# Fetching the next expert's token rows from memory instead of gathering them with matrix products

## The reference

```python
logits = (h @ w_router).astype(jnp.float32)
top_val, top_idx = lax.top_k(logits, TOP_K)
top_w = jax.nn.softmax(top_val, axis=-1)
combine = jnp.sum(jax.nn.one_hot(top_idx, N_EXPERTS) * top_w[..., None], axis=-2)
for e in range(N_EXPERTS):
    y = (jax.nn.silu(h @ w_gate[e]) * (h @ w_up[e])) @ w_down[e]
    out = out + combine[..., e:e + 1] * y
```

## Time and profile before

| what | value |
|---|---|
| median of 3 runs | 1670.8 us (1670.58 to 1673.57) |
| profiled execution, its own time | 1674.03 us |
| its span, first to last instruction | 1672.2 us |
| granted TensorE clock, mean | 0.992 |
| TensorE busy | 1622.5 us, 97% |
| VectorE / ScalarE / GpSimd busy | 578.3 / 501.1 / 49.1 us |
| bytes moved by DMA | 469.96 MB |
| experts, first to last part | 701 to 1655.5 us, 120.2 us from one to the next |

### The profile page before, as it was taken

How to read it: one execution, slowest core, us unless ns; L and a number is a source line. 1 busy time by engine, 2 the same in 40 slices (tenths; PEclk the granted TensorE clock), 3 DMA queues, 4 the chain that set the end, 5 groups by cost and what they waited for, 6 DMA issues and landing times.

```text
span 1672.2 us, 29242 instructions
## 1 busy us (share of the span) xinstructions
PE 1622.5 (97%) x12632; PEld 884.4 (53%) x12632; DVE 578.3 (35%) x820; ACT 501.1 (30%) x745; POOL 49.1 (3%) x33
## 2 busy tenths in 40 slices
PE   6998999999999899999999999999999999999996
PEld 5877788888887777633334334234333333333332
DVE  5877676556787767300100100100100110110101
ACT  5687655444558855300000000000100110010001
POOL 0130000000013000000000000000000000000000
PEclk9999999999999999999999999999999999999998
DMA  9433365555543434399999999999999999999994
GB/s 374 152 130 147 112 241 201 184 185 198 177 164 126 146 132 166 123 385 381 348 370 378 347 376 378 345 388 360 374 376 357 357 391 352 358 385 368 359 386 165
DMA packets 65898, 469.96 MB, mean 281 GB/s; under 512 B 7280, under 2 KB 7536, under 8 KB 9712
## 3 DMA queue, kind: packets, MB, share of 16 engines
q1 hardware_dynamic: 64480, 460.88, 72.5%
q0 software_dynamic: 864, 6.29, 1.0%
q10 hardware_dynamic: 432, 0.96, 0.1%
HBM read 467.05 MB, written 1.05 MB: 280 GB/s over the span
## 4 chain that ended last, share of the span: by engine, by line
PE 81%; DVE 8%; ACT 6%; issue 2%; DMA 1%; SPq 0%; DVEq 0%; ACTq 0%
PE bank L1289 25%; PE turn L1303 12%; PE mid L1289 10%; PE turn L1309 6%; PE bank L503 5%; PE bank L504 5%; PE bank L505 5%; DVE w_lo L498 2%; PE mid L503 2%; PE mid L505 2%; PE mid L504 2%; ACT w_hi L491 2%; PE bank L1201 2%; DMA raw<-in_stream 1%; DVE xT L1542 1%
## 5 line engine op out<-in xcount | busy, mean ns | idle before, releaser
L1289 PE MATMUL bank<-raw,gT 128*32 128x512 f32 (+1 forms) x4096 | 443.5, 567 | 0.8 <-ACT gT L919 0.8
L498 DVE TENSOR_TENSOR w_lo<-raw,w_hi 128x1024 fp32r<-128x1024 f32 x202 | 253.9, 1267 | 154.5 <-ACT w_hi L491 152.8
L1289 PEld LDWEIGHTS bank<-raw,gT 128*32 128x32 f32 x4096 | 129.1, 110 | 265.5 <-issue 255.7
L503 PE MATMUL bank<-w_hi,a_hi 128*128 128x512 f32 (+1 forms) x608 | 242.8, 399 | 15.5 <-DVE w_lo L498 12.0
L491 ACT ACTIVATE w_hi<-raw 128x1024 fp32r<-128x1024 f32 x202 | 211.3, 1056 | 128.0 <-PE bank L505 81.0
L504 PE MATMUL bank<-w_lo,a_hi 128*128 128x512 f32 (+1 forms) x608 | 234.7, 386 | 0.0
L505 PE MATMUL bank<-w_hi,a_lo 128*128 128x512 f32 (+1 forms) x608 | 234.3, 385 | 0.0
L1303 PE MATMUL turn<-raw,hT 128*32 128x512 f32 x1792 | 213.5, 594 | 0.0
L1289 PE MATMUL mid<-raw,gT 128*32 128x256 f32 (+1 forms) x2048 | 188.6, 486 | 0.0
L940 ACT ACTIVATE eh<-bank 128x512 f32<-128x512 f32 (+1 forms) x32 | 17.4, 544 | 455.9 <-PE bank L1289 291.5
L503 PEld LDWEIGHTS bank<-w_hi,a_hi 128*128 128x128 f32 x608 | 116.4, 191 | 41.8 <-issue 15.0
(11 more groups left out here) (226 smaller groups left out, 1377.3 us busy)
## 6 DMA issues: line engine op xcount, KB each, us to landing
raw<-in_stream SPq DMA_DIRECT2D x436, 1024.0 KB, 6.9
wg<-in_gates POOLq DMA_DIRECT2D x2, 2048.0 KB, 10.3
gain<-in_norms POOLq DMA_DIRECT2D x4, 512.0 KB, 4.3
x<-in_x SPq DMA_DIRECT2D x2, 512.0 KB, 6.9
raw<-in_stream SPq DMA_DIRECT2D x2, 512.0 KB, 6.9
out_x<-xn SPq DMA_DIRECT2D x4, 256.0 KB, 2.0
const<-in_consts ACTq DMA_DIRECT2D x1, 752.0 KB, 11.7
gain<-in_norms SPq DMA_DIRECT2D x2, 256.0 KB, 7.1
```

What stands on the lines that cost most here:

```text
L498: nc.vector.tensor_tensor(w_lo[:, h % H, :], raw[:, part % R, lo:lo + HALF], w_hi[:, h % H, :].bitcast(F32), ALU.subtract).then_inc(lo_rea ...
L503: nc.tensor.matmul(out_, s_hi, wh, start=start, stop=False)
L1289: ins = nc.tensor.matmul(bank_[strip(s_), 0:w], gT[:, kt, strip(t_)], w_c, start=kt == 0, stop=kt == KT - 1)
```

## The change

The scaled tokens `xs` are written once to a tensor `tokens` in the chip's memory by GpSimd. For each next expert, TensorE multiplies `sel` with a column that holds each token's number plus one (`number`; two products with one moving column), before part 33. VectorE subtracts one, clips at zero and writes the result as whole numbers into `index` (96 places). GpSimd waits for that, then issues an indirect DMA that fetches 96 rows of 4 KB into `fetched`. Before part 40 TensorE waits for the rows and turns them with 8 transposes into the same PSUM banks as before; ScalarE copies them to `gT` as before. The gather by products stays for expert 0. Places without a token fetch row 0, where the gather gave zeros; `selT` has no column that uses them.

```diff
-AT_GATHER = [N_IN + 6, N_IN + 8]
+AT_INDEX = N_IN + 5
+AT_GATHER = N_IN + 12
...
+            fetched = keep("fetched", [P, D], into=m)
...
+            pool.wait_ge(xs_ready, 2 * TB)
+            pool.dma_start(tokens.rearrange("(b p) d -> p b d", p=P), xs[:, :, :]).then_inc(stored, 16)
+            pool.wait_ge(stored, 16)
+            def fetch(n, e):
+                pool.wait_ge(index_ready, n + 1 + e)
+                nc.gpsimd.indirect_dma_start(fetched[0:CAP, :], None, tokens,
+                                             bass.IndirectOffsetOnAxis(ap=index[0:CAP, 0:1], axis=0)).then_inc(rows_landed, 16)
+            for e in range(EXPERTS - 1):
+                if e:
+                    pool.wait_ge(g_full, 2 * (e + 1))
+                fetch(FETCHES[0], e)
...
-                        for j, at_ in enumerate(AT_GATHER):
-                            if i == at_ and not is_last(pas, e):
-                                if j == 0:
-                                    pe.wait_ge(sel_ready, TB * (c0 + 2) + e * TB)
-                                    pe.wait_ge(hT_top, q0 + len(QUADS) + e * len(QUADS))
-                                    pe.wait_ge(hT_rest, q0 + len(QUADS) + e * len(QUADS))
-                                gather(j)
+                        if i == AT_INDEX and not is_last(pas, e):
+                            pe.wait_ge(sel_ready, TB * (c0 + 2) + e * TB)
+                            pe.wait_ge(number_s, 3)
+                            pe.wait_ge(selT_ready, pas * EXPERTS + 2 + e)
+                            for b in range(TB):
+                                ins = nc.tensor.matmul(early[2][0:CAP, T:T + 1], sel[:, b, :], number[:, b:b + 1],
+                                                       start=b == 0, stop=b == TB - 1)
+                            ins.then_inc(index_full, 1)
+                        if i == AT_GATHER and not is_last(pas, e):
+                            pe.wait_ge(hT_top, q0 + len(QUADS) + e * len(QUADS))
+                            pe.wait_ge(hT_rest, q0 + len(QUADS) + e * len(QUADS))
+                            pe.wait_ge(rows_landed, 16 * (FETCHES[pas] + 1) + e * 16)
+                            for kt in range(KT):
+                                ins = nc.tensor.transpose(early[kt // 4][:, kt % 4 * CAP:(kt % 4 + 1) * CAP],
+                                                          fetched[0:CAP, kt * P:(kt + 1) * P], ident[0:CAP, 0:CAP])
+                                if kt == 3:
+                                    ins.then_inc(g_full, 1)
+                            ins.then_inc(g_full, 1)
...
+            nc.vector.tensor_reduce(number[:, 0:1], before, AX.X, ALU.add).then_inc(number_s, 1)
+            dve.wait_ge(number_s, 1)
+            nc.vector.tensor_scalar(number[:, 1:2], number[:, 0:1], -1.0, 2.0 * P, ALU.mult,
+                                    ALU.add).then_inc(number_s, 1)
+            dve.wait_ge(number_s, 2)
+            nc.vector.tensor_scalar(number[:, 0:1], number[:, 0:1], -1.0, 1.0 * P, ALU.mult,
+                                    ALU.add).then_inc(number_s, 1)
             dve.wait_ge(logit_full, 1)
             nc.vector.tensor_copy(lgT[:, :], mid[0:EXPERTS, 0, 0:T]).then_inc(logit_rows, 1)
...
                         select(column(e + 2))
+                        dve.wait_ge(index_full, FETCHES[pas] + 1 + e)
+                        nc.vector.tensor_scalar(index[0:CAP, :], early[2][0:CAP, T:T + 1], -1.0, 0.0, ALU.add,
+                                                ALU.max).then_inc(index_ready, 1)
```

More of the change, by code:

```diff
@@ L276, with build @@
 V_END = V_ROUTER + KT * EXPERTS
-def build(nc, stream, gates_w, x_in, norms, consts_in, vecs_in, out):
+def build(nc, stream, gates_w, x_in, norms, consts_in, vecs_in, out, tokens):
     with ExitStack() as ctx:
@@ L348, in build @@
             selT = keep("selT", [P, T], F32R, m)
-            keep("sel_end", [P, 64], into=m)
+            number = keep("number", [P, TB], into=m)
+            index = keep("index", [P, 1], I32, m)
+            keep("sel_end", [P, 61], into=m)
             rw = keep("rw", [P, 2, KT * EXPERTS], F32R, m)
@@ L456, in build @@
         slot_turned = sem("selection_turned")
+        number_s = sem("token_number_parts")
+        stored = sem("tokens_stored")
+        index_full = sem("row_numbers_summed")
+        index_ready = sem("row_numbers_ready")
+        rows_landed = sem("expert_rows_landed")
         selT_ready = sem("selection_rows_ready")
@@ L560, in each_expert @@
                     yield e
+        FETCHES = [0, EXPERTS - 1, 2 * EXPERTS - 1]
         def column(e):
@@ L695, in _ @@
             pool.wait_ge(s_gain, 16 * 2 * DEPTH)
+            pool.wait_ge(xs_ready, 2 * TB)
[9 more added lines that the diff above has]
+                fetch(FETCHES[0], e)
+            pool.wait_ge(route_ready, 1)
+            n = pool.value_load(most_i[0:1, 0:1], min_val=0, max_val=T)
+            with pool.If(n > CAP):
+                for pas in (1, 2):
+                    for e in range(EXPERTS):
+                        pool.wait_ge(g_full, 2 * (ROUNDS[pas] + 1) + e * 2)
+                        fetch(FETCHES[pas], e)
         @block.scalar
@@ L1279, in experts @@
                             if (q, k0) == (0, 0):
+                                if not is_first(pas, e):
+                                    pe.wait_ge(index_ready, FETCHES[pas] + e)
                                 pe.wait_ge(g_ready, 2 * (c0 + 1) + e * 2)
@@ L1879 @@
     out = nc.dram_tensor("out_x", (T, D), F32, kind="ExternalOutput").ap()
-    build(nc, *aps, out)
+    tokens = nc.dram_tensor("tokens", (T, D), F32, kind="Internal").ap()
+    build(nc, *aps, out, tokens)
     r = run_bass_kernel_spmd(nc, [{f"in_{k}": a for k, a in arrays.items()}], core_ids=[0])
```

## The result

| | before | changed |
|---|---|---|
| median | 1671.05 us (1670.58 to 1673.57, 4 runs) | 1652.65 us (1651.35 to 1655.86, 4 runs) |
| profiled execution, own time / span | 1674.03 / 1672.2 us | 1653.23 / 1651.3 us |
| one inner expert | 120.2 us | 117.53 us |

The ratio is 0.9886, 95% interval [0.9874, 0.9898]: 18.4 us faster, with an interval of 17.0 to 21.1 us. Forecast were 1654.3 us and 16.5 us.

A forecast was written before the change was run, and what follows sets the result against it. The prediction took TensorE to bound the experts. Its terms, −29.0 + 7.6 + 4.2 + 0.7 = −16.5 us, took the median of 1670.8 us to 1654.3 us, with a range of 1650.2 to 1663.7 us.

The forecast's parts named there:

- TensorE's list is the time of an expert: In the experts, TensorE is busy in all of 120.2 us; work taken off its list comes off the end.
- Gather −29.0 us: Experts 1 to 7: removing the gather products saves 4.14 us each, −29.0 us.
- Transposes +7.6 us: Before part 40: eight added transposes cost 1.09 us in each of seven experts, +7.6 us.
- the low bound of 0.8 us: Lowest cost predicted for the group of eight transposes before part 40; the high bound was 2.07 us.
- Index products +4.2 us: Before part 33: two added index products cost 0.6 us in each of seven experts, +4.2 us.
- Lead-in +0.7 us: At the routing: three VectorE instructions ahead of the logit copy, not hidden, cost +0.7 us once.
- Fetch 0: Between index products and transposes: rows land within the 18.1 us of parts 33 to 39, no wait, 0.
- the rival: Rows come late: TensorE waits before part 40, costing 7 x (L − 17.7) for landing after L us; chance 0.07.
- Stream 0: Weight stream in the experts: 44.4 MB at 377 GB/s, below the 388 and 406 GB/s seen, costs 0.
- nearer to 8 or 9 us: Down parts: weight loads should land this long after issue, against 12.9 us allowed.
- a limiting stream: Experts: 367 GB/s is all memory gives on average, 121 us an expert, 1677 us; chance 0.04.
- a partial loss: Experts: the fetch delays weight loads and TensorE stands 1 us an expert, 1661 us; chance 0.09.

The follow-up runs named there:

- fetch_unused: Changed kernel with the gather by products put back before parts 34 and 36, the fetch kept but its rows unused: 1676.15 us, ratio to the kernel before 1.0027.
- turn_ahead: Changed kernel with number_early, the selection turned one expert ahead and VectorE summing row numbers instead of the first pass's index products: 1648.9 us, ratio to before 0.986.
- number_early: Changed kernel with the three VectorE token-numbering steps moved to where router weights are split: runs of 1652.04, 1652.55 and 1655.2 us, and an outlier of 9367 us.
- late8: Changed kernel with the transposes of fetched rows moved from before part 40 to before part 36: 1677.3 us, ratio to the kernel before 1.0034.
- spread5: Changed kernel with five more fetches an expert, issued apart during the next expert's parts 2 to 22: 1653.4 us.
- extra3: Changed kernel with three more fetches of the same rows an expert, in a row behind the real one, read by nothing: 1666.5 us (one run).
- spread3: Changed kernel with three more fetches an expert, issued apart when TensorE has used parts 4, 14 and 24 of the next expert: 1652.7 us.

## Why the prediction was right, point by point

- *TensorE's list is the time of an expert.* Right. TensorE is busy in all of 117.53 us, and fetch_unused and turn_ahead moved the time by what they put on and took off the list.
- *Gather −29.0 us.* Its price could be read from before alone, and fetch_unused, which puts the gather back, confirms it to 0.03 us an expert. The sum closes on the medians to 0.3 us, within their interval.
- *Transposes +7.6 us.* 7 x 0.93 = 6.5 us. The term was 0.16 us a group too high: the group of 128 and 64 moved columns was the right kind of row, and 0.93 us lie about halfway between it and the low bound of 0.8 us.
- *Index products +4.2 us.* 7 x 0.54 = 3.8 us. The cost to enter was taken a little high.
- *Lead-in +0.7 us.* 0.55 us, shown to be on the path by number_early. The small steps took 0.15 us each.
- *Fetch 0.* Right, by a cover that is real: landing took 8.5 to 10.1 us, between the two rows of GpSimd's loads although it moves less than the smaller of them, and late8 shows what three parts of cover would have given. The price in the rival, seven times the wait, was right but for the clock falls behind two of the waits.
- *Stream 0.* The term was right. Its ground was half right: the rates of the earlier trace rows are an average room, and spread5 confirms it; they say nothing of a burst, nor that a fetched byte takes more DMA time than a streamed one. I forecast landing "nearer to 8 or 9 us" against 12.9, and the loads issued around the fetch did that:

```profile
raw<-in_stream SPq DMA_DIRECT2D x7, 1024.0 KB, 8.6
fetched<-tokens,index POOLq DMA_INDIRECT x1, 9.8
```

(The view of DMA from 1020 to 1040 us; issues, size, median us to landing.) So about 4 us were left, and extra3 shows that three more fetches there use them up. The rivals of a limiting stream and a partial loss fall for this kernel.

All small errors lay on the same side, 1.6 us together, which is the distance of 16.5 from 18.1 us. The sum closes because the mechanism does, in the trace and in fetch_unused; the last tenths of the medians prove nothing.

## What to carry to other kernels

Where one engine is busy throughout a stage, price an edit of its list by differences of start times around a like group, with and without it; the busy times of single instructions overlap. Move work to an idle engine or a DMA if its result is due late enough, and count the cover in parts of the loop: here 17.9 us from the index to the transposes, against 10.6 us to the landing. Against a prefetched stream, judge an added transfer by the DMA time that it takes beside the slack of the loads in flight, and not by average bandwidth: the same bytes cost 14 us in a row behind the real fetch and nothing apart.

## What the runs showed that I had not expected

- 0.39 MB fetched by index take 8.5 to 10.1 us from issue to landing beside the stream, and GpSimd is busy for only 0.9 us of it.
- A DMA share of 1.00 is no sign of a limit: spread3 and spread5 stand at it without loss, at 390 and 396 GB/s, extra3 with loss, at 381.
- 0.39 MB fetched by index take 1.5 us of the time of all DMA engines, in which the stream moves 0.6 MB.
- A wait of TensorE can be followed by a granted clock of 1.2 GHz: in late8, for some 3.3 us behind two of seven waits, of 3.4 and 2.8 us, and not behind another of 2.8 us.
